# A hybrid block with a second mixer: the compressed attention branch's hidden layer starts one step later and is spread over four more steps

## The reference, cut to what matters

```python
def compress(x, pe, w1, w2):
    blk = x[:, cmp_idx] + pe[None, None, :, None, :]
    blk = jnp.transpose(blk, (0, 1, 3, 2, 4)).reshape(B, n_cmp, G, CMP_LEN * Dh)
    hid = jax.nn.gelu(jnp.einsum('bngi,ih->bngh', blk, w1))
    return jnp.einsum('bngh,ho->bngo', hid, w2)
...
s = jnp.einsum('bqghd,bngd->bghqn', qb, k_cmp) * scale
p_cmp = masked_softmax(s, cmp_end[None, :] <= tq[:, None])
o_cmp = jnp.einsum('bghqn,bngd->bqghd', p_cmp.astype(dt), v_cmp)
...
o = gb[..., 0:1] * o_cmp + gb[..., 1:2] * o_slc + gb[..., 2:3] * o_win
```

## Time and profile before

| | |
|---|---|
| Time of three runs, median | 1692.33 us (1691.41 to 1694.46) |
| Time of the profiled execution | 1691.58 us |
| Span of the profile | 1689.8 us |
| Mean granted clock of TensorE | 0.991 of full speed |
| Busy: TensorE, VectorE, ScalarE | 96%, 57%, 47% of the span |
| The chain of `hidr`, first layer | from 1402.3 to 1411.9 us |
| The chain of `hidr`, second layer | from 1584.2 to 1593.7 us |

### The profile page before, as it was taken

One profiled execution on the slowest core, in us unless ns is written; L12 is line 12 of the kernel. 1 busy time (PEld: TensorE's weight loads), 2 busy tenths in 40 slices (PEclk: granted clock), 3 DMA queues, 4 the chain that ended last, 5 costly groups with the idle time before them and its releaser, 6 DMA issues. The chain is left out here.

```text
span 1689.8 us, 23056 instructions
## 1 busy us (share of the span) xinstructions
PE 1630.5 (96%) x8818; PEld 1378.0 (82%) x8818; DVE 960.7 (57%) x1399; ACT 788.7 (47%) x1246; POOL 149.9 (9%) x180
## 2 busy tenths in 40 slices
PE   7999999999999999999999999999999998999897
PEld 5888799877878887888889977778887777878686
DVE  4555564344665545555455444565554677767675
ACT  4444354445354444444355444554443444444443
POOL 0000012211200000000012111210000200010000
PEclk9999999999999999999999999999999999999999
DMA  7665455343455555655545443355655543244421
GB/s 255 206 205 197 156 192 167 131 131 113 156 186 183 191 183 166 202 193 177 181 159 186 139 134 111 131 188 192 202 187 162 174 147 132 69 160 143 150 94 50
DMA packets 77581, 273.76 MB, mean 162 GB/s; under 512 B 8608, under 2 KB 9632, under 8 KB 77472
## 3 DMA queue, kind: packets, MB, share of 16 engines
q1 hardware_dynamic: 77472, 272.30, 48.9%
HBM read 271.21 MB, written 1.05 MB: 161 GB/s over the span
## 5 line engine op out<-in xcount | busy, mean ns | idle before, releaser
L289 DVE TENSOR_TENSOR wlo<-raw,whi 128x1024 fp32r<-128x1024 f32 (+4 forms) x468 | 559.6, 1200 | 428.9 <-ACT whi L283 404.2
L283 ACT ACTIVATE whi<-raw 128x1024 fp32r<-128x1024 f32 (+3 forms) x496 | 510.0, 1032 | 474.2 <-PE bank L339 456.5
L337 PE MATMUL bank<-whi,hh 128*128 128x512 f32 (+4 forms) x1312 | 498.0, 380 | 9.9 <-DVE wlo L289 8.5
L339 PE MATMUL bank<-whi,hl 128*128 128x512 f32 (+4 forms) x1312 | 487.1, 371 | 0.0
L338 PE MATMUL bank<-wlo,hh 128*128 128x512 f32 (+4 forms) x1312 | 486.6, 371 | 0.0
L337 PEld LDWEIGHTS bank<-whi,hh 128*128 128x128 f32 x1312 | 248.6, 189 | 54.1 <-ACT whi L283 7.5
L339 PEld LDWEIGHTS bank<-whi,hl 128*128 128x128 f32 x1312 | 248.1, 189 | 40.4
L338 PEld LDWEIGHTS bank<-wlo,hh 128*128 128x128 f32 x1312 | 248.7, 190 | 36.0
L337 PE MATMUL bank<-hh,whi 128*128 128x256 f32 x480 | 145.2, 302 | 0.0
L339 PE MATMUL bank<-whi,gl 128*128 128x512 f32 x352 | 140.3, 399 | 0.0
L337 PE MATMUL bank<-whi,gh 128*128 128x512 f32 x352 | 138.8, 394 | 0.0
(11 more groups left out here) (288 smaller groups left out, 1743.0 us busy)
## 6 DMA issues: line engine op xcount, KB each, us to landing
raw<-W SPq DMA_DIRECT2D x464, 512.0 KB, 3.4
raw<-W SPq DMA_DIRECT2D x26, 384.0 KB, 3.6
gbc<-gains SPq DMA_DIRECT2D x10, 512.0 KB, 4.6
raw<-W SPq DMA_DIRECT2D x8, 416.0 KB, 3.0
tab<-tab SPq DMA_DIRECT2D x6, 384.0 KB, 3.9
raw<-W SPq DMA_DIRECT2D x4, 426.0 KB, 3.1
raw<-W SPq DMA_DIRECT2D x6, 192.0 KB, 3.1
x<-x_in SPq DMA_DIRECT2D x2, 512.0 KB, 5.6
```

The lines of the kernel that those rows point to most:

```text
L283: high = act.op(lambda e: e.activation(whi[i][:, 0:w], r[:, 0:w], ACT.Copy), self.landed[c], free)
L289: tok = (low or dve).op(lambda e: e.tensor_tensor(wlo[i][:, 0:w], r[:, 0:w], whi[i][:, 0:w].bitcast(F), ALU.subtract), self.landed[c], hig ...
L337: pe.op(lambda e: e.matmul(dst, ah, bh, start=start, stop=False), *tokens, mark=False)
L339: return pe.op(lambda e: e.matmul(dst, al, bh, start=False, stop=stop), mark=mark)
```

## The change

Four pauses of `compressed` become longer: a new step before the square, two instead of one after it, two instead of one between the product and the tanh, and three instead of two before the transposes. Nothing is computed differently; all later steps of `compressed` are emitted four ticks later.

```diff
                 i, src, tok = toks["hid"]
                 c = math.sqrt(2 / math.pi)
+                yield
                 e = a_fn(hidr[:, :, :], src, ACT.Square, tok, base)
-                yield
+                yield from pause(2)
                 d = ts(dve, hidr[:, :, :], hidr[:, :, :], 0.044715 * c, c, ALU.mult, ALU.add, e)
                 d = tt(dve, hidr[:, :, :], hidr[:, :, :], src, ALU.mult, d)
-                yield
+                yield from pause(2)
                 e = a_fn(hidr[:, :, :], hidr[:, :, :], ACT.Tanh, d)
                 yield from pause(2)
                 toks["gelu"] = stt(hidr[:, :, :], hidr[:, :, :], 1.0, src, ALU.add, ALU.mult, e)
                 M2.give(i, toks["gelu"])
-                yield from pause(2)
+                yield from pause(3)
                 i, bank, free = XB.take()
```

## The result

The changed kernel takes 1702.2 us (median of four runs, 1700.62 to 1703.49) against 1693.13 us for the kernel before on the same chips: a ratio of 1.0054 with a 95% interval of 1.0041 to 1.0067. It is slower by 9 us; the forecast was 1690.8 us, between 1686.5 and 1697. The profiled execution of the changed kernel has a span of 1698.8 us, of the kernel before 1689.8. Busy times are those of the earlier trace rows to within 0.3%, with one exception to keep in mind: GpSimd is busy for 4.0 us more, with the same 180 instructions.

What follows compares the result with a forecast made beforehand. TensorE, busy 96% of the span, was taken as the bound. Per layer 3.7 us gained up to the output products less 3.0 at the layer's end gave 0.7, 1.5 for both: 1690.8 us, range 1686.5 to 1697, no visible difference.

Steps and rivals of the forecast that it cites:

- the gain at `hidr`: At the hidr links, TensorE's 1.69 and 2.81 us waits shrink or go; next wk transposes come 5.4 us sooner.
- Three pairs on: Three pairs after hidr, the wk transposes of 1434.19 come at 1429.7, 4.5 us sooner, with a 2.1 us TensorE wait.
- The chain of 15.1 us: From nmt through exponentials, copy, whi, wlo and nmt again to the transposes of 1434.19: 15.1 us, 15.28 before.
- the end of the layer: Late oc addition and gate products make the qTh product start 3.0 us late, with oc and qTl waits of 2.6 together.
- the moved products of `kcv`: Behind the transposes three pairs on, kcv products still come and give back 0.6 us, leaving 3.9 gained.
- the softmax of `cw`: Its VectorE operations crowd in front of fql, on which the first output products wait; 0.2 us lost.
- rival (a): Clock falls at the new gaps, about 2.8 us each: slower, two falls 1696.4 us, four 1702; chance 0.25.
- The stretch from 1308: Evidence cited against clock falls: there TensorE was busy 2.05 of 4.00 us, yet the clock stayed at 1.00.

Runs made afterwards that it cites:

- e2: Kernel before with four ticks more behind vbd only (pause 7 instead of 3); 1702.73 us, ratio to before 1.0065.
- e5: Changed kernel with eight small chained GpSimd operations put before the kcv rotation; 1701.81 us, ratio to before 1.0055.
- e8: As e6, but the six kcv rotation operations done by VectorE instead of GpSimd; 1695.38 us, ratio to before 1.0015.
- e9: Changed kernel with the kcv transposes one tick later, taken back right behind them; 1696.84 us, ratio to before 1.0029.
- e11: Changed kernel with its four ticks taken back behind the kcv transposes, one at each of four later pauses; 1689.53 us, ratio to before 0.9985.
- e4: Changed kernel with the gate product of half 0 ahead of two wlo instead of behind them; 1697.06 us, ratio to before 1.0027.
- e6: Changed kernel with four ticks taken back behind the kcv transposes: one ahead of vbd, two behind, one after cw scores; 1697.54 us, ratio to before 1.0038.
- e7: As e6, but kcv transposes one tick later, taken back between the cw scores of the two halves; 1684.69 us, ratio to before 0.9953.
- e10: As e7, but the tanh one tick later, behind the copy of wk on ScalarE; 1683.71 us, ratio to before 0.9949.
- h6: TensorE order of e7, but hidr operations on VectorE and ScalarE where the kernel before has them; 1686.67 us, ratio to before 0.9967.
- e1: Changed kernel with its four ticks taken back from behind the kcv rotation on, ahead of the kcv transposes too; 1695.19 us, ratio to before 1.0014.

## Why the prediction was wrong

**Right: the gain at `hidr`.** I said that the `wk` transposes of 1416.93 come 5.4 us sooner, with a wait of 2.0 us for the copy behind the tanh. They came 5.5 and 5.6 sooner, with 1.95 and 1.96. Three pairs on I said 4.5; it was 4.75 and 4.9. The chain of 15.1 us, which I had named as the likeliest to upset the sum, took 15.05 (from `nmt` at 1413.33 to the transposes at 1428.38).

**Right: the end of the layer.** I said 3.0 us late by two waits of 2.6 together. It was 3.35 with 1.04 and 1.50, and e2 shows the same 3.35 alone. Both terms were a little too small: from the transposes to the product it takes 2.15 us where I took 2.01, and the rest is 1.20 where I had 1.0.

**Wrong, the step "the moved products of `kcv`": 0.6 us.** I priced the products and not what they wait for. The six rotation operations on GpSimd lay before in a stretch in which VectorE was idle. The change moves them beside three taps, and they take 3.5 instead of 1.6 us, which TensorE feels as a wait of 1.25 (e5, e8, e9). The 0.6 for the products was nearly right. By their starts they take 0.16 (the transpose, 1430.29 to 1430.45) and 0.41; as a remainder it is 0.85, for e11, which has the wait and one fall of 3.4 us, needs 3.8 us more than before from the transposes three pairs on to `whi,fqh`, and 3.8 − 1.25 − 1.7 leaves 0.85. I had read which engine does the rotation and not asked what its neighbour does meanwhile.

**Nearly right: the softmax of `cw`.** I put 0.2. In the same stretch e11 is 0.4 us shorter than the changed kernel in the first layer (39.61 against 40.00, one fall each); that is the price. The wait for `cw` itself grew from 0.32 to 1.58 us, but the 0.77 us for `fql` behind it went.

**Wrong, the choice against rival (a).** The clock fell at new gaps: behind the wait for `kcv` (1.7 us of cost in the first layer, 3.4 in the second) and at the end of each layer (1.6 us by the last row of the first table). Both places were named with the price of a fall; I gave it a quarter. For the first gap, ahead of the `wk` transposes at 1410.39, rival (a) is wrong too: the clock fell there in the first layer and it cost nothing, since a wait behind it shrank from 2.0 to 0.5 us. In the second layer it did not fall there (1.00 from 1596 to 1600). That rival (a) names 1702 us for four falls, the measured time, is luck: it priced a fall at 2.8 us, while the four that counted cost 1.7, 3.4, 1.6 and 1.6, 8.3 in all, and it had no wait for `kcv`.

The sum per layer in the first: −5.5 + 0.7 + (1.25 + 1.7 + 0.8 + 0.4) + 3.35 + 1.6 = +4.3, as measured. My sum was −5.4 + 0.9 + 0.6 + 0.2 + 3.0 = −0.7. Of the 5.0 us between them 3.3 are two clock falls and 1.25 is the rotation. In the second layer the fall behind `kcv` was twice as long.

By the Trainium skill ("TensorE: Matmul & The Clock Gate", section "HAM oscillation — how this bites in real kernels") the waits for data between groups of products brought the low clock back each time in the kernel that it describes. Here the falls of the changed kernel do stand behind such waits, but not every wait brings one. Behind the 1.25 us for `kcv` the clock fell in all ten layers that have this wait (changed, e4, e5, e6, e11), and in one of the ten without it (e7, e8, e9, e10, h6; it is the second layer of e8, where the clock fell behind the wait of 2.00 us for the copy of `wk`). The same 1.04 and 1.50 us at the end of the layer were followed by a fall in the changed kernel, e5 and e9 but not in e2; e2 and e9 fell at `cw`, and the changed kernel did not. The stretch from 1308, which I held against rival (a), is no evidence either way: with the same instructions and the same wait the clock stayed up in the kernel before and fell in e11 (and e10). The wait and the stretch behind it, e11 and then before:

```profile
1310.76 1.11 PE L347 MATMUL bank<-kc,wk 128*128 128x128 f32 x4 [2.21 <-DVE wk L365]
1311.00:1313.00 2.00, 2.00 (x8) 1.71 (x8) 1.90 (x3) 1.09 (x3) 0.00 (x0) 0.50 0.05 18
```

```profile
1309.95 0.66 PE L347 MATMUL bank<-kc,wk 128*128 128x128 f32 x4 [2.21 <-DVE wk L365]
1311.00:1313.00 2.00, 2.00 (x10) 1.61 (x9) 1.23 (x3) 2.00 (x6) 0.37 (x3) 1.00 0.48 119
```

So neither the order of the instructions nor the length of a wait settles whether a fall follows. Why it is one or the other stays open; I did not find a rule that I could have used.

## What to carry to other kernels

Delaying one side chain delays all that hangs on it. Take the ticks back at the first point where the chain has slack (e7_kct_late against the changed kernel: 17.5 us for pauses alone), and look at every cross-engine step of it on its way, with what the neighbouring engines do there. Where two kernels differ by small waits, count the falls of the clock first: a wait of 1.25 us cost 3 to 4.7 with its fall (1.25 and 1.7 or 3.4), and a fall inside a stretch that another engine sets cost nothing. Of the four repairs e1, e6, e7 and e11 two made a new wait of their own, so a moved step needs its profile too.

## What was unexpected of the hardware

A GpSimd operation of 15x16 elements takes 0.21 us when VectorE is idle or reads PSUM, and as long as VectorE's work where that has two SBUF inputs: 1.17 and 1.08 us beside `wlo`, 1.52 and 1.42 beside three taps. The latter ran one behind the other, and GpSimd's operation ended only 0.08 us behind the third. By the Trainium skill ("SBUF — State Buffer", section "SBUF: two separate sides") the two share one pair of ports as an exclusive lock, for a VectorE operation with two SBUF inputs against a GpSimd operation that reads SBUF, and whoever comes second waits for the whole instruction. The runs agree on which operations get in each other's way, but not on the rest. By the profile the first rotation operation started 0.18 us ahead of the taps (1426.75 against 1426.93 in the changed kernel) and still waited, and over three of them, while VectorE's taps took their usual 0.47 us. It is not always so: in e5 an added operation that started at 1425.85, beside two taps in a row, ended 0.08 us behind the first. What decides between the two is not shown.

Where the clock fell within D it stayed low for 3.4 or 6.8 us at a time, but for the 17 us in e1_early_tail. With one and the same order of TensorE (e7, e10, h6) the low clock came to 6.8, 0 and 3.4 us within D.
